# Where in a partition the split weights and the later buffers begin: a change of byte positions alone

## The reference

```python
x = x + hybrid_mixer(rmsnorm(x, norm_mix), w_in, ..., w_br, w_out)     # three token mixers, merged by gates
x = x + memory_cross_attention(rmsnorm(x, norm_xa), rmsnorm(mem, norm_mem), wq, wkv, wo, gq, gk)
x = x + conv_glu_ffn(rmsnorm(x, norm_ffn), w_up, w_conv, w_down)       # 2048 -> 2 x 5632 -> 2048
```

## Time and profile before

| what | value |
|---|---|
| median of three runs | 2003.33 us (2003.0 to 2004.33) |
| span of the profiled execution | 2001.0 us |
| TensorE, matmuls | 1987.1 us busy (99%), 14,790 instructions |
| TensorE, weight loads | 1895.9 us busy (95%), 14,790 |
| VectorE | 1216.1 us (61%) |
| ScalarE | 892.0 us (45%) |
| granted TensorE clock over the span | 1.000 |
| DMA | 382.65 MB, mean 191 GB/s |

### The profile page before, as it was taken

How to read it: one execution, slowest core, us unless ns; L and a number is a source line. 1 busy time by engine, 2 the same in 40 slices (tenths; PEclk the granted TensorE clock), 3 DMA queues, 4 the chain that set the end, 5 groups by cost and what they waited for, 6 DMA issues and landing times.

```text
span 2001.0 us, 34706 instructions
## 1 busy us (share of the span) xinstructions
PE 1987.1 (99%) x14790; PEld 1895.9 (95%) x14790; DVE 1216.1 (61%) x1352; ACT 892.0 (45%) x877; POOL 40.5 (2%) x62
## 2 busy tenths in 40 slices
PE   8999999999999999999999999999999999999999
PEld 8999999999999999999999999988888888888888
DVE  5677645445454476576655345777777777754444
ACT  5445334434364343455434344544444444433333
POOL 1000100000000000000000000000000000000000
PEclk9999999999999999999999999999999999999999
DMA  8766754665557766565564456665656565566664
GB/s 268 220 192 195 226 159 143 198 200 166 182 174 247 243 198 223 169 194 186 178 199 129 139 168 198 212 208 171 207 171 206 173 204 174 177 205 223 185 203 134
DMA packets 356637, 382.65 MB, mean 191 GB/s; under 512 B 8144, under 2 KB 351604, under 8 KB 355124
## 3 DMA queue, kind: packets, MB, share of 16 engines
q1 hardware_dynamic: 350947, 353.36, 55.9%
q0 software_dynamic: 5584, 27.70, 4.0%
HBM read 367.47 MB, written 13.58 MB: 190 GB/s over the span
## 4 chain that ended last, share of the span: by engine, by line
PE 97%; DVE 1%; ACT 1%; DMA 0%; issue 0%; SPq 0%; DVEq 0%; ACTq 0%
PE bank L1961 18%; PE bank L1962 18%; PE bank L1963 18%; PE bank L1998 16%; PE bank L2000 8%; PE bank L2473 8%; PE bank L2474 4%; PE bank L2381 1%; PE bank L2400 1%; PE bank L2158 1%; DVE w_lo_home L1131 1%; ACT w_hi_home L540 0%; PE bank L2204 0%; PE bank L2061 0%; PE bank L2152 0%; DMA ident<-in_shape_masks 0%
## 5 line engine op out<-in xcount | busy, mean ns | idle before, releaser
L1131 DVE TENSOR_TENSOR w_lo_home<-raw,w_hi_home 128x2048 fp32r<-128x2048 f32 (+1 forms) x349 | 756.7, 2168 | 606.2 <-ACT w_hi_home L540 605.8
L540 ACT ACTIVATE w_hi_home<-raw 128x2048 fp32r<-128x2048 f32 (+2 forms) x359 | 645.0, 1798 | 1047.5 <-PE bank L1963 624.3
L1961 PE MATMUL bank<-x_home,w_hi_home 128*128 128x256 f32 x2304 | 648.1, 281 | 1.9 <-DVE w_lo_home L1131 1.9
L1962 PE MATMUL bank<-x_home,w_hi_home 128*128 128x256 f32 x2304 | 643.1, 279 | 0.0
L1963 PE MATMUL bank<-x_home,w_lo_home 128*128 128x256 f32 x2304 | 642.8, 279 | 0.0
L1998 PE MATMUL bank<-x_home,w_hi_home 128*128 128x512 f32 x1408 | 488.5, 390 | 0.1
L1961 PEld LDWEIGHTS bank<-x_home,w_hi_home 128*128 128x128 f32 x2304 | 433.1, 188 | 2.8 <-DVE w_lo_home L1131 1.4
L1962 PEld LDWEIGHTS bank<-x_home,w_hi_home 128*128 128x128 f32 x2304 | 433.2, 188 | 0.2
L1963 PEld LDWEIGHTS bank<-x_home,w_lo_home 128*128 128x128 f32 x2304 | 433.0, 188 | 0.0
L2000 PE MATMUL bank<-x_home,w_lo_home 128*128 128x256 f32 x1408 | 397.0, 282 | 0.0
L1998 PEld LDWEIGHTS bank<-x_home,w_hi_home 128*128 128x128 f32 x1408 | 264.2, 188 | 55.7 <-issue 0.4
(11 more groups left out here) (315 smaller groups left out, 1942.4 us busy)
## 6 DMA issues: line engine op xcount, KB each, us to landing
raw<-in_w_in SPq DMA_DIRECT2D x52, 2048.0 KB, 8.4
raw<-in_ffn_up SPq DMA_DIRECT2D x44, 2048.0 KB, 8.0
raw<-in_ffn_down SPq DMA_DIRECT2D x32, 1408.0 KB, 6.6
raw<-in_xa_wkv SPq DMA_DIRECT2D x16, 2048.0 KB, 9.3
raw<-in_w_br SPq DMA_DIRECT2D x8, 2048.0 KB, 8.4
raw<-in_w_out SPq DMA_DIRECT2D x8, 2048.0 KB, 8.3
raw<-in_xa_wq SPq DMA_DIRECT2D x8, 2048.0 KB, 8.3
raw<-in_xa_wo SPq DMA_DIRECT2D x8, 2048.0 KB, 8.4
```

Source lines behind the costliest of these rows:

```text
L540: return nc.scalar.activation(out_, in_, func, **kw)
L1131: tt(split_out(w_lo, kind, half), halves(raw, kind, half, par), split_out(w_hi, kind, half).bitcast(f32), ALU.subtract).then_inc(lo_ready, 1)
L1961: mm(o, w[0], x[0], start=start, stop=False)
L1962: mm(o, w[0], x[1], start=False, stop=False)
```

## The change

The stationary and the moving weights get one and the same place, 24 float32 elements (96 bytes) into their homes, in all stages. An unused buffer of 64 elements (256 bytes) is declared ahead of `xT`, so `xT` and every buffer after it lie 256 bytes later. Nothing else is altered: every engine has the same instructions on the same operands in the same order, and only byte positions differ (line numbers move by one or two).

```diff
+W_AT = 24
 ...
         w_hi_home = sb("w_hi_home", [P, 2, KC * P + 64], f32r)
         w_lo_home = sb("w_lo_home", [P, 2, KC * P + 64], f32r)
-        w_hi, w_lo = w_hi_home[:, :, 0:KC * P], w_lo_home[:, :, 0:KC * P]
-        wt_hi, wt_lo = w_hi_home[:, :, 16:16 + KC * P], w_lo_home[:, :, 16:16 + KC * P]
+        w_hi, w_lo = (t[:, :, W_AT:W_AT + KC * P] for t in (w_hi_home, w_lo_home))
 ...
         small = sb("small", [P, 128])
+        gap = sb("gap", [P, 64])
         r_scope = ExitStack()
         xT = sb("xT", [P, KC, SEQ], f32, r_scope)
 ...
             if kind == TM_:
-                return (wt_hi if tile is w_hi else wt_lo)[:, half, :]
+                return tile[:, half, :]
 ...
-                        w = [t[:, half, k * CW:(k + 1) * CW] for t in (wt_hi, wt_lo)]
+                        w = [t[:, half, k * CW:(k + 1) * CW] for t in (w_hi, w_lo)]
```

## The result

The changed kernel takes 2010.56 us, median of 15 runs (2004.46 to 2015.34); beside it the kernel before takes 2003.82 us (2003.0 to 2004.75, 15 runs). The ratio is 1.0032, 95% interval 1.0025 to 1.0039: slower by 6.7 us. Beside the median the spread has changed, from 1.75 to 10.9 us. The profiled execution is the longest of the 15 (2015.34 us, span 2013.3 us), so its surplus of 12.3 us over the span of before is larger than that of the median.

A forecast was written before the change was run, and what follows sets the result against it. TensorE's matmul pace was taken as the bound, busy 1987.1 of 2001.0 us. Strip, engine writes and weights summed 0 + 0 + 0, leaving a 2001.0 us span; with 2.3 us to the median, 2003.3 us, range 1980 to 2036 us.

The forecast's parts named there:

- What bounds the kernel: Whole kernel: TensorE's matmuls are busy 1987.1 of 2001.0 us, so the time follows their pace.
- The strip at 0: Buffers moved by the 256 unused bytes: priced at 0, as BR against Z and DN against UP agree to 0.1 ns.
- ScalarE and VectorE at 96 at no cost: Writes of the split weights at 96 bytes: same durations as at 0 and 64, any slowdown lost in slack, cost 0.
- The weights at 96: I take 0: Matmul operands in all stages, now 64 bytes apart instead of 32: term 0, bounded by 46 us lost and 132 us gained.
- the upper bound that the prediction had for them: UP and DN: at most 14 us lost, from the gate columns' 3.3 ns per matmul at distance 0, on 4,224 matmuls.
- The reason given for 0: Operand distances: of 32 and 0 only 0 costs more, and 64 is farther from 0 than 32 is.
- Three stretches agree on 116.7 ns: Z, BV and BR before the change: different operand places, the same 116.7 ns a matmul, so placement was priced at 0.
- slower: All 256-column matmuls: distance 64 collides like 0, 3.3 ns each, 2035 us (2049 if UP and DN pay fully); chance 0.28.
- its sign to look for: Z and BV: a pace of 120 ns a matmul would show the slower rival.
- Faster: Matmuls at distance 64 beat 32: 3.3 ns on 9,696 gives 1971 us, half a step on all 1980; chance 0.32.
- The 109.2 ns: 256-column matmuls: the Trainium skill's gap formula, columns / 2.4 + 2.5 ns, an estimate that would gain 73 us on 9,696.

The follow-up runs named there:

- the places chosen by these readings: Changed kernel with weights at 0 in BO, GB, WO, Q, XO, UP and DN, at 64 bytes in V: 1994.26 us, ratio 0.9954.

## Why the prediction was wrong

The time lies inside the range given, but the forecast was no change, and the kernel is slower by 0.32% (0.25 to 0.39%). That it is no more is luck: a loss of 14 us and a gain of about 7, of which the forecast had neither, partly cancel. By the prediction's own steps:

- **What bounds the kernel**: right. TensorE is still busy 99%, its waits stay at a few us, and the whole difference is pace.
- **The strip at 0**: right, shown by the kernel that has it alone (0.9999) and, with the weights at 96, by the one that lacks it (2010.62 us against 2010.56).
- **ScalarE and VectorE at 96 at no cost**: right. In Z of the changed kernel their instructions take 1922 and 2293 ns; before 1917 and 2292.

```profile
L1132 DVE TENSOR_TENSOR w_lo_home<-raw,w_hi_home 128x2048 fp32r<-128x2048 f32 x6 | 13.8, 2293 | 5.5 <-ACT w_hi_home L541 5.5
...
L541 ACT ACTIVATE w_hi_home<-raw 128x2048 fp32r<-128x2048 f32 x6 | 11.5, 1922 | 16.9 <-PE bank L1964 16.9
```

- **"The weights at 96: I take 0"**: this is the step that failed. It holds two terms, and neither is 0. For UP and DN it is +6.7 ns a pair, 14.1 us, shown both ways by taking those stages out (-13.8 us) and by changing them alone (+14.0 us over the 2004.01 of the kernel before beside it). That sits at the upper bound that the prediction had for them (14 us), but not by its mechanism: only the step after the matmul of 512 columns is longer (235.0 against 228.4 ns), and in the same stages distance 0, where the bound came from, costs nothing once settled. For the triples the term is -3.3 or +1.1 ns from half to half, about -7 us in the median: the kernel with UP and DN back at 0 stands at 1996.8 against 2004.0.
- **The reason given for 0**, that only distance 0 costs and 64 is farther from it than 32: it falls. The paces do not grow smoothly from a bad place; each place has its own one to three for triples, and pairs have others: at distance 64 and at 96 and 48 they lose what they do not lose at 0.
- **"Three stretches agree on 116.7 ns"**: the stretches were too few. The trace of before already held a second pace for one and the same place. K, rows of the timeline before:

```profile
870.04 0.28 PE L1961 MATMUL bank<-mem_hl,w_hi_home 128*128 128x256 f32 x1
...
885.95 0.28 PE L1961 MATMUL bank<-mem_hl,w_hi_home 128*128 128x256 f32 x1
```

  135 steps at 117.9 ns, with the operands at (0, 32) as in Z; later in K it is 116.7 again. Read half by half, it would have shown that pace has a memory, and that a number for a place is not enough. The 116.7 ns themselves are two patterns with one mean: in Z of before the steps are 116 and 117 ns, in BR they run from 113 to 120.
- **The rivals**: "slower" had the sign, and its place (UP and DN, both bounded at 14 us) but not its sign to look for: no triple runs at 120 ns. "Faster" named a step of 3.3 ns, which is what several stages show, and its size, 1980 us or less, needs all stages to hold that pace; the best version timed more than once, that with the places chosen by these readings, reached 1994.3. The 109.2 ns that the prediction gives beside that rival were not reached either: the best settled pace in any run is 113.3.

What stays open is why a place has the paces it has (that two reads meet, as both rivals supposed, no run shows), what chooses one after a pause, and the 120.0 ns in BR.

## What to carry to other kernels

Where TensorE is the bound and runs float32r matmuls back to back, as here, the byte places of its two operands count: they moved this kernel between 1991 and 2028 us, 1.8%, and single stages between 113.3 and 123.3 ns a matmul. A place should be tuned for each shape of matmul by itself: what gained here for 256 columns lost twice as much for 512. Read the pace start to start and half by half over the whole program before trusting one number, and time a change of places over many runs, because a pace once taken is held and a short pause can choose another.

## What was not expected of the hardware

Steady paces come in a few fixed values (113.3, 116.7, 117.3, 117.8, 118.3, 118.8, 120.0, 123.3 ns for 256 columns at the granted clock of 2.4 GHz), hold for a hundred matmuls and more without a change, and two or three of them exist for the same instructions at the same places. The Trainium skill (TensorE: Matmul & The Clock Gate, "Step-by-step: what each phase is for") says that the read ports of the moving operand and of the weight load are independent, so that loading the next weights takes no read bandwidth from the running matmul. By that rule places would not count. Here they do: with nothing but `x_hl` 32 bytes farther, BV went from 116.7 to 120.0 ns and BO to 113.3. Whether the two reads meet there, no run shows. And a pace 3% faster in GC ran into the loads of the weights in both kernels that had it at that place, with a wait of 0.83 and 0.84 us that neither the kernel before nor the changed one has in GC.
